# Moving the meta query's scores of a head from the head ahead (slots 4 to 6) into the head itself (slots 1 and 2)

## The chip, the core and the metric

The kernel runs on one core of one Trainium2 chip. The metric is the device time of one execution in microseconds (us); of several executions the median counts. The core has five engines with a queue each: TensorE (PE, with its weight loads shown apart as PEld), VectorE (DVE), ScalarE (ACT), GpSimd (POOL) and SyncE (SP), which here only issues DMAs. An engine runs its instructions in the order of the program and waits at semaphores for the others.

## What is computed

One layer of a bidirectional encoder over 1024 tokens with 16 meta tokens in front (1040 positions, 1024 features). Cut to the part that matters here:

```
q = rope(rmsnorm((rmsnorm(c_q) @ w_uq).reshape(B, T, 8, 96)))
k = rope(rmsnorm(concat(k_nope, k_rope)))           # 8 heads, 96 wide
s = einsum('bqhd,bkhd->bhqk', qblk, k) * scale      # T = 1040 keys
p = softmax(s, axis=-1)
y_mla = einsum('bhqk,bkhd->bqhd', p, v)
y = concat(rmsnorm(y_lru * gelu(g_lru)), rmsnorm(y_mla))
h = h + y @ w_out
gate, up = split(rmsnorm(h) @ w_ffn_up)
h = h + (silu(dwconv(gate)) * up) @ w_ffn_down
return h[:, 16:]                                     # meta rows are dropped
```

Only the 1024 token rows leave the layer, but the convolution over positions in the last part needs the row before the first token. That row is a meta position, so the attention also has to be done for the last meta tokens' queries; two of them are taken ("the meta query").

## The kernel before

The program has a projection and LRU part, an attention part (from about 245 to 535 us), the output projection, and the feed-forward part. The change is in the attention part, in `attention_out_phase`.

**Heads and slots.** There are 8 heads (0 to 7; END is 7) of 9 slots (0 to 8), one slot for each 128 keys; slot 8 holds the 16 meta keys. The loop `for h, s in steps` runs over heads and slots on PE, ACT and DVE alike. The numbers are fp32 split into a high and a low part, so each product takes three matmuls. In slot s PE makes

1. the scores of the keys of slot s against 512 queries (3 matmuls, L2027 to L2029), then a side job at place 0,
2. the scores against the other 512 queries (3 matmuls), then a side job at place 1,
3. the first half of the products with v of slot s-2 (3 matmuls, L2047, L2048, L2050; for slot 8 one matmul, L2044), then a side job at place 2,
4. the second half of these (3 or 1), then a side job at place 3.

ACT in slot s does the side jobs of places 0 and 1, in slot 1 the copy of the last head's output (`read_output`, o_sb, L1523), then two exponentials of the scores (e_f L1554 and e_h L1561; for slot 8 e_f, L1558 and L1559), and after them the side jobs of places 2 and 3. In slot 0 of heads 1 to 4 it also squares a part of y (L1482). DVE makes the low parts e_l of the last slot's exponentials (L1737, one for each half) between its share of the side jobs.

**Side jobs.** A side job writes one PSUM bank with PE, and ACT or DVE reads it. `PREPARE` lists them by slot and place, for head h+1 while head h runs: tq0, tq1, tk0, tk1 transpose q and k (four transposes each, L1907; ACT copies the high part, L1427, and then DVE makes the low part, L1141); a0 to a15 and am give the row maximum (one matmul L1922, DVE reduces it, L1699); tm transposes the meta rows (L1911, ACT L1437 and L1439); r transposes the maxima into a row (L1929), which ACT copies (L1448) and SP sends into row 96 of q_h. The scores of slot 0 wait for that row. x0, x1 and x2 are the meta query's scores: three matmuls each (L1941 to L1943), 2 rows against 512, 512 and 16 keys; ACT copies each into x_one (L1458); when x2 is copied, SP sends x_one to the head's rows of x_all (L1320). x_all is first read in slot 1 of head 7.

**Banks and waits.** In the heads the side jobs take two PSUM banks in turn, in the order of their list (`side_of`, `before`): the side job n waits on PE until the job n-2 has been read by its reader, which is ACT for x0, x1, x2 and r, and DVE for tq, tk and a. An a job also waits until ACT has copied the high parts of q and k of its head (`side_hi`). `read_output` waits for the last product of the last head, the second L2044 (`pv_done`).

**SP.** For each head SP has in its queue, in this order: (from head 1 on) the wait for x2 and x_all's DMA, the wait for r and the row's DMA, and `recip_row` of the last head (the sums' row out of o_sb as soon as o_sb is copied, L1162; then DVE's reciprocal at the end of slot 4; then two more DMAs).

Of the kernel before, what the change touches and what calls it, by code (L numbers as in the profile page):

```python
# [81 lines left out]
def f32(ap):  # L82
    return ap.bitcast(F32)
# [940 lines left out]
def attention_out_phase(nc, place, con, qk, v, yl, ym, res_t, x_h, x_l, up_raw, s_h, s_l, halo, bank, dram, sem):  # L1024
# [41 lines left out]
    def s_ps(g):  # L1066
# [7 lines left out]


    PREPARE = {0: ("tq0", "", "", "tq1"), 1: ("", "tk0", "", ""), 2: ("tk1", "", "a0", "a1"), 3: ("a2", "a3", "a4", "tm"),
               4: ("a5", "x0", "a6", "a7"), 5: ("a8", "x1", "a9", "a10"), 6: ("a11", "x2", "a12", "a13"),
               7: ("a14", "a15", "am", "r"), 8: ("", "", "", "")}
    FIRST = dict(PREPARE)
    FIRST.update({4: ("a5", "", "a6", "a7"), 5: ("a8", "", "a9", "a10"), 6: ("a11", "", "a12", "a13"), 8: ("x0", "x1", "x2", "")})  # L1080
    META_QUERIES = {5: ("xt", "", "", ""), 8: ("", "", "", "xo")}
    LRU_SUMS = {1: ("ys", "", "", "")}
    END = HEADS - 1
    NONE = ("", "", "", "")

    def side_jobs(h, s):

        places = [None] * 4
        for plan, head in [(FIRST if h < 0 else PREPARE, h + 1), (META_QUERIES, h), (LRU_SUMS, h)]:
            if 0 <= head < HEADS and not (plan is META_QUERIES and h != END) and not (plan is LRU_SUMS and h != END - 2):  # L1090
                for i, kind in enumerate(plan.get(s, NONE)):
                    if kind:
                        assert places[i] is None
                        places[i] = (kind, head)
        return places

    steps = [(h, s) for h in range(-1, HEADS + 1) for s in range(SLOTS)]
    jobs = [j for h, s in steps for j in side_jobs(h, s) if j]
    number = {j: n for n, j in enumerate(jobs)}
    first = len([j for s in range(SLOTS) for j in side_jobs(-1, s) if j])  # L1100
    BY_ACT = {"r", "x0", "x1", "x2"}
    LOWS = [("tq0", 0), ("tq1", 0), ("tk0", 0), ("tk1", 0)]
# [29 lines left out]
    def wait_read(eng, j):  # L1132

        same = [i for i in jobs[:number[j] + 1] if by_act(i) == by_act(j)]
        eng.wait_ge(sem["side_read_act" if by_act(j) else "side_read_dve"], len(same))
# [23 lines left out]
    def recip_row(eng, h):  # L1159

        eng.wait_ge(sem["o_read"], h + 1)
        eng.dma_start(rs, o_sb[VD:VD + 1].rearrange("p (a b) -> p a b", b=XT)).then_inc(sem["sums_in"], 16)  # L1162
        eng.wait_ge(sem["sums_recip"], h + 1)
        eng.dma_start(dram["recip"].rearrange("(a b) -> a b", b=XT), rs).then_inc(sem["recip_row"], 16)
        eng.wait_ge(sem["recip_row"], 16 * (h + 1))
        if h:
            eng.wait_ge(sem["y_mul"], h)
        eng.dma_start(rb, dram["recip"].unsqueeze(0).broadcast_to([VD, SEQ])).then_inc(sem["recip_in"], 16)
# [69 lines left out]
    def upto(kind, t):  # L1238

        return XT + 1 + GROUPS.index((kind, t)) + 1  # L1240
# [33 lines left out]
    def raw_of(m):  # L1274
        return raw03 if m == 3 else raw0[m % 4] if m < KD else raw1[m - KD]
# [35 lines left out]
    def sync(sp):  # L1311
        for h in range(HEADS):

            if h == END:
                sp.wait_ge(sem["ysum"], 4)
                for k in range(4):
                    sp.dma_start(raw_of(k), dram["w_out"][P * k:P * k + P, 0:half]).then_inc(sem["wo_a"][k], 16)
            def last_queries():
                wait_read(sp, ("x2", h))
                sp.dma_start(x_all[2 * h:2 * h + 2], x_one).then_inc(sem["x_in"], 16)  # L1320

            if h:
                last_queries()
            wait_read(sp, ("r", h))
            sp.dma_start(f32(q_h[h % 2][QK:QK + 1, 0:SEQ].rearrange("p (t n) -> p t n", n=P)), f32(r_row))\
              .then_inc(sem["row_in"], 16)
            if h == 0:
                last_queries()
            if h == END:
                sp.wait_ge(sem["side_done"], number[("tm", END)] + 1)  # L1330
                for i in range(4):
                    sp.dma_start(res_t[:, i, :], dram["x_tm"][P * i:P * i + P, :]).then_inc(sem["res_a"], 16)
            if h:
                recip_row(sp, h - 1)
        for i in range(4, XT):
            sp.dma_start(res_t[:, i, :], dram["x_tm"][P * i:P * i + P, :]).then_inc(sem["res_b"], 16)
        sp.wait_ge(sem["s_done"], SLOTS * END)
        for k in range(LF, KD):
            sp.wait_ge(sem["wo_lo"], k - LF + 1)
            sp.dma_start(raw0[k % 4], dram["w_out"][P * k:P * k + P, 0:half]).then_inc(sem["wo_a"][k % 4], 16)  # L1340
        sp.wait_ge(sem["s_done"], G)
        for k in range(LF):
            sp.dma_start(raw1[k], dram["w_out"][P * k:P * k + P, half:]).then_inc(sem["wo_in"][k], 16)
        recip_row(sp, END)

        sp.wait_ge(sem["wo_mm"], XT)
        sp.wait_ge(sem["wo_lo"], KD)
        for k in range(LF, KD):
            sp.dma_start(raw1[k], dram["w_out"][P * k:P * k + P, half:]).then_inc(sem["wo_a"][k - LF], 16)
        sp.dma_start(hm, dram["meta_tm"][META - 2:META, :]).then_inc(sem["res_in"], 16)  # L1350
        sp.dma_start(fg, dram["ffn_g"]).then_inc(sem["res_in"], 16)
        sp.wait_ge(sem["wo_lo"], 2 * KD)
        sp.dma_start(up_raw[:, 0, :], dram["w_up"][0, 0]).then_inc(sem["up_in"][0], 16)
        sp.wait_ge(sem["wo_mm"], upto("M", XT))
        for b in range(1, 4):
            sp.dma_start(up_raw[:, b, :], dram["w_up"][0, b]).then_inc(sem["up_in"][b], 16)
# [58 lines left out]
    def scalar(act):  # L1415
# [109 lines left out]
        for h, s in steps:  # L1525
# [10 lines left out]
            if h >= 1 and s == 2:  # L1536
                if h == HEADS - 1:

                    act.wait_ge(sem["x_max"], 1)
                    nc.scalar.activation(x_row, x_all, ACT.Exp, bias=x_v[QK:QK + NX, 3, 0:1], scale=SCALE)\  # L1540
                      .then_inc(sem["x_act"], 1)
            js = side_jobs(h, s)
            for j in js[0:2]:
                if j:
# [557 lines left out]
    def tensor_end(pe):  # L2102
        for n in blocks_in(NT)[1:]:
            transpose_block(pe, n)

    return {"sync": sync, "gpsimd": gpsimd, "scalar": scalar, "vector": vector, "tensor": tensor,
            "scalar_end": scalar_end, "tensor_end": tensor_end, "hn_meta": hn_m, "groups": ALL}

# [894 lines left out]
def build(nc, dram, out):  # L3003
    with ExitStack() as ctx:
# [21 lines left out]
        x_h, x_l, up_raw, s_h, s_l = norm_maps(place)  # L3026
        halo = place("halo", con["late"], (KD,))
        attention = attention_out_phase(nc, place, con, qk, v, yl, ym, h, x_h, x_l, up_raw, s_h, s_l, halo, bank, dram, sem)
        ffn = ffn_phase(nc, place, con, attention["hn_meta"], attention["groups"], h, x_h, x_l, up_raw, s_h, s_l, halo, bank, dram, out, sem)
        with nc.Block() as block:  # L3030
# [108 lines left out]
```

## Time and profile before

| | us |
|---|---|
| device time, median of 3 executions (lowest, highest) | 1303.34 (1301.97, 1305.87) |
| span of the profiled execution, first to last instruction | 1302.3 |
| PE busy in it | 1268.3 (97%) |
| DVE busy | 987.3 (76%) |
| ACT busy | 775.5 (60%) |
| POOL busy | 147.3 (11%) |
| share of PE in the chain that ended last | 86% |

The span leaves out what the chip does before the first and after the last instruction; the device time of the profiled execution itself is not listed apart, and the median of the executions is 1.0 us above its span. Busy time is the sum of an engine's instructions. Matmuls overlap: one of 512 columns is shown with some 0.39 us, but the next one begins 0.23 us after it. So PE's real pace is read from the starts, and the idle time in brackets in a timeline is counted from the modelled end of the matmul before it.

### The profile page before, as it was taken

The page shows a single profiled execution, that of the slowest core. Times are in us where ns is not written, and L with a number is a line of the kernel's source. Part 1 is how long each engine was busy: PE and PEld are TensorE (multiplying, and loading weights), DVE is VectorE, ACT ScalarE, POOL GpSimd, SP SyncE. Part 2 cuts the span into 40 slices and gives each one's busy share as a digit, 9 for nine tenths or more (in the row PEclk, how much of TensorE's full clock was granted, in tenths as well). Part 3 has the DMA queues.
Part 4 walks back from the last instruction along what each step waited for, and adds up shares of the span by engine and source line. Part 5 has one row for each costly group of instructions (what it writes and reads, how often), then busy time and mean ns, then how long its engine had stood idle before and what let it go on. Part 6 is the DMA issues. An engine that isn't in the chain of part 4 may idle for free.

```text
span 1302.3 us, 18506 instructions
## 1 busy us (share of the span) xinstructions
PE 1268.3 (97%) x6158; PEld 1015.7 (78%) x6158; DVE 987.3 (76%) x1498; ACT 775.5 (60%) x1163; POOL 147.3 (11%) x175
## 2 busy tenths in 40 slices
PE   7999999899999999999999999999999999999998
PEld 7999997666666666587678888888888888888886
DVE  6677569677777776577789887887878887887855
ACT  7487648567666776534445665656474665656460
POOL 3000037400000001232200000000010000000010
PEclk9999999999999999999999999999999999999999
DMA  6111200000000014210144847576674847575667
GB/s 220 35 52 41 74 1 1 1 2 9 9 9 10 9 42 170 62 37 1 37 148 103 190 97 169 112 170 133 158 165 93 193 97 169 110 169 132 161 138 250
DMA packets 40937, 123.00 MB, mean 94 GB/s; under 512 B 7378, under 2 KB 8082, under 8 KB 34484
## 3 DMA queue, kind: packets, MB, share of 16 engines
q0 software_dynamic: 7200, 52.43, 21.2%
q1 hardware_dynamic: 33684, 69.86, 15.5%
q8 instruction: 33, 0.54, 0.2%
q14 instruction: 20, 0.16, 0.0%
HBM read 62.34 MB, written 59.80 MB: 94 GB/s over the span
## 4 chain that ended last, share of the span: by engine, by line
PE 86%; ACT 5%; DVE 5%; issue 2%; DMA 1%; POOL 0%; SPq 0%; DVEq 0%; ACTq 0%; POOLq 0%
PE banks L2898 31%; PE banks L2970 15%; PE banks L100 7%; PE banks L102 7%; PE banks L101 7%; PE banks L1922 2%; PE banks L2027 2%; PE banks L2028 2%; PE banks L2029 2%; PE banks L2047 2%; PE banks L2050 2%; PE banks L2048 2%; ACT e_h L1561 1%; ACT e_f L1554 1%; PE banks L1882 1%
## 5 line engine op out<-in xcount | busy, mean ns | idle before, releaser
L2898 PE MATMUL banks<-x_hi,slot_h 128*128 128x512 f32 x616 | 242.9, 394 | 2.5 <-DVE slot_l L2586 1.3
L2898 PE MATMUL banks<-x_lo,slot_h 128*128 128x512 f32 x616 | 243.4, 395 | 0.0
L2898 PE MATMUL banks<-x_hi,slot_l 128*128 128x512 f32 x616 | 242.9, 394 | 0.0
L2371 ACT ACTIVATE slot_h<-up_raw 128x512 fp32r<-128x512 f32 x127 | 79.9, 630 | 174.2 <-PE banks L2898 173.5
L2898 PEld LDWEIGHTS banks<-x_hi,slot_h 128*128 128x128 f32 x616 | 115.6, 188 | 31.0 <-DVE slot_l L2586 2.3
L2898 PEld LDWEIGHTS banks<-x_lo,slot_h 128*128 128x128 f32 x616 | 115.7, 188 | 27.1
L2898 PEld LDWEIGHTS banks<-x_hi,slot_l 128*128 128x128 f32 x616 | 115.7, 188 | 26.9
L2449 ACT ACTIVATE staged<-banks 128x1024 f32<-128x1024 f32 x100 | 101.6, 1027 | 41.0 <-PE banks L2970 41.0
L2970 PE MATMUL banks<-dn_h,a_h 128*128 128x512 f32 x280 | 110.4, 394 | 0.0
L2970 PE MATMUL banks<-dn_h,a_l 128*128 128x512 f32 x280 | 109.5, 391 | 0.0
L2970 PE MATMUL banks<-dn_l,a_h 128*128 128x512 f32 x280 | 109.5, 391 | 0.0
L2354 POOL DMA_DIRECT2D down_sums<-staged x50 | 44.3, 886 | 570.3 <-ACT staged L2449 495.4
L1699 DVE TENSOR_REDUCE lam_t<-banks 128x1 f32<-128x512 f32 x128 | 85.3, 683 | 22.4 <-PE banks L1922 22.0
L100 PE MATMUL banks<-xn_h,win_h 128*128 128x346 f32 (+5 forms) x304 | 96.4, 317 | 1.5 <-DVE xn_l L669 1.5
L102 PE MATMUL banks<-xn_h,win_l 128*128 128x346 f32 (+5 forms) x304 | 95.2, 313 | 0.0
L101 PE MATMUL banks<-xn_l,win_h 128*128 128x346 f32 (+5 forms) x304 | 95.1, 313 | 0.0
L1554 ACT ACTIVATE e_f<-banks 128x1024 f32<-128x1024 f32 (+1 forms) x72 | 73.7, 1023 | 35.3 <-PE banks L2029 34.8
L1737 DVE TENSOR_TENSOR e_l<-e_f,e_h 128x512 fp32r<-128x512 f32 x128 | 88.0, 697 | 1.9 <-ACT e_h L1561 1.8
L2586 DVE TENSOR_TENSOR slot_l<-up_raw,slot_h 128x512 fp32r<-128x512 f32 x127 | 86.8, 684 | 3.2 <-ACT slot_h L2371 3.2
L2729 DVE SCALAR_TENSOR_TENSOR gate_conv<-gate,par,gate_conv 128x1024 f32<-128x1024 f32 x44 | 55.5, 1283 | 24.8 <-ACT gate_conv L2463 20.4
L1561 ACT ACTIVATE e_h<-banks 128x1024 fp32r<-128x1024 f32 x64 | 65.4, 1021 | 0.0
L1922 PE MATMUL banks<-k_h,q_h 96*128 96x512 f32 x128 | 54.8, 430 | 9.6 <-ACT k_h L1427 8.1
(345 smaller groups left out, 2848.2 us busy)
## 6 DMA issues: line engine op xcount, KB each, us to landing
down_sums<-staged POOLq DMA_DIRECT2D x50, 1024.0 KB, 8.0
up_raw<-in_w_up SPq DMA_DIRECT2D x88, 256.0 KB, 3.2
dn_raw<-in_w_down SPq DMA_DIRECT2D x22, 512.0 KB, 6.7
win_raw<-in_w_in SPq DMA_DIRECT2D x11, 512.0 KB, 3.3
x_tm<-in_x_tm SPq DMA_DIRECT2D x8, 512.0 KB, 6.0
wo_raw<-in_w_out SPq DMA_DIRECT2D x16, 256.0 KB, 4.2
h<-in_x_tm SPq DMA_DIRECT2D x8, 512.0 KB, 5.6
down_sums<-h SPq DMA_DIRECT2D x3, 1024.0 KB, 6.7
```

The source lines that it names most:

```text
L100: nc.tensor.matmul(out, w_h, x_h, start=first, stop=False)
L101: nc.tensor.matmul(out, w_h, x_l, start=False, stop=False)
L102: return nc.tensor.matmul(out, w_l, x_h, start=False, stop=last)
L1554: nc.scalar.activation(e_f[g % 3][0:n], s_ps(g)[0:n], ACT.Exp, scale=SCALE)
L1699: ins = nc.vector.tensor_reduce(mx3[:, i:i + 1], side, AX.X, ALU.max)
L1737: nc.vector.tensor_tensor(e_l[(g - 1) % 2][:, cs], e_f[(g - 1) % 3][:, cs], f32(e_h[(g - 1) % 3][:, cs]), ALU.subtract).then_inc(sem["e_lo ...
L1922: ins = nc.tensor.matmul(side, q_h[b][0:QK, tile_of(t)], k_h[b][0:QK, 512 * c:512 * c + 512], start=True, stop=True)
L2371: nc.scalar.activation(s_h[slot], x, ACT.Copy).then_inc(sem["up_hi"], 1)
L2449: nc.scalar.activation(staged[b][:, 2 * p:2 * p + 2, :], bank(4 + 2 * p, 2).rearrange("p (i n) -> p i n", i=2), ACT.Copy).then_inc(sem["dn ...
L2586: nc.vector.tensor_tensor(s_l[slot], x, f32(s_h[slot]), ALU.subtract).then_inc(sem["up_lo"], 1)
L2898: ins = nc.tensor.matmul(o, s[slot][:, k], xs[w], start=fresh and k == 0 and n == 0, stop=k == 3 and n == 2, skip_group_check=not fresh)
L2970: ins = nc.tensor.matmul(bank(4 + i), x[:, ts], w, start=k in FRESH and n == 0, stop=n == 2, skip_group_check=k not in FRESH)
```

## The change

x0, x1 and x2 of heads 1 to 6 leave places 1 of slots 4, 5 and 6 of the head ahead. They now stand in the head itself: x0 at place 2 and x1 at place 3 of slot 1, x2 at place 1 of slot 2. Head 0 (made ahead of the loop) and head 7 (made in slots 4 to 6 of head 6, `LAST_AHEAD`) stay as they were. The instructions are the same and as many as before. On SP the row's DMA of a head now stands ahead of x_all's DMA, and `recip_row` behind it.

```diff
     PREPARE = {0: ("tq0", "", "", "tq1"), 1: ("", "tk0", "", ""), 2: ("tk1", "", "a0", "a1"), 3: ("a2", "a3", "a4", "tm"),
-               4: ("a5", "x0", "a6", "a7"), 5: ("a8", "x1", "a9", "a10"), 6: ("a11", "x2", "a12", "a13"),
+               4: ("a5", "", "a6", "a7"), 5: ("a8", "", "a9", "a10"), 6: ("a11", "", "a12", "a13"),
                7: ("a14", "a15", "am", "r"), 8: ("", "", "", "")}
+    LAST_AHEAD = dict(PREPARE)
+    LAST_AHEAD.update({4: ("a5", "x0", "a6", "a7"), 5: ("a8", "x1", "a9", "a10"), 6: ("a11", "x2", "a12", "a13")})
     FIRST = dict(PREPARE)
-    FIRST.update({4: ("a5", "", "a6", "a7"), 5: ("a8", "", "a9", "a10"), 6: ("a11", "", "a12", "a13"), 8: ("x0", "x1", "x2", "")})
+    FIRST.update({8: ("x0", "x1", "x2", "")})
+    OWN = {1: ("", "", "x0", "x1"), 2: ("", "x2", "", "")}
...
-        for plan, head in [(FIRST if h < 0 else PREPARE, h + 1), (META_QUERIES, h), (LRU_SUMS, h)]:
+        ahead = FIRST if h < 0 else LAST_AHEAD if h == END - 1 else PREPARE
+        for plan, head in [(ahead, h + 1), (META_QUERIES, h), (LRU_SUMS, h), (OWN, h)]:
+            if plan is OWN and not 1 <= h < END:
+                continue
...
-            if h:
+            if h == END:
                 last_queries()
             wait_read(sp, ("r", h))
             sp.dma_start(f32(q_h[h % 2][QK:QK + 1, 0:SEQ].rearrange("p (t n) -> p t n", n=P)), f32(r_row))\
               .then_inc(sem["row_in"], 16)
-            if h == 0:
+            if h != END:
                 last_queries()
```

Line numbers after the change are 4 higher near PREPARE and 6 higher behind it.

PE, slots 1 and 2 of head 1, before (the transposes L1907 are tk0 and, in the second place, tk1; `side_read_dve` and `side_read_act` are the waits for a bank's reader):

```order
L1907 MATMUL banks<-ident,qk 96x128 [waits side_read_dve]
L1907 MATMUL banks<-ident,qk 96x128 x3
L2044 MATMUL banks<-e_meta,v_meta 66x512 [waits e_lo,e_hi]
L2044 MATMUL banks<-e_meta,v_meta 66x512 [waits e_lo]
L2027 MATMUL banks<-q_h_131,k_h_135 128x512 [waits e_hi]
L2028 MATMUL banks<-q_l_133,k_h_135 128x512
L2029 MATMUL banks<-q_h_131,k_l_137 128x512
L1907 MATMUL banks<-ident,qk 96x128 [waits side_read_dve]
```

and with the change (L1947 to L1949 are x0 and x1, L2050 is the product with v that was L2044, L1913 is tk1):

```order
L2050 MATMUL banks<-e_meta,v_meta 66x512 [waits e_lo,e_hi]
L1947 MATMUL banks<-k_h_135,q_h_131 2x512 [waits side_read_dve]
L1948 MATMUL banks<-k_h_135,q_l_133 2x512
L1949 MATMUL banks<-k_l_137,q_h_131 2x512
L2050 MATMUL banks<-e_meta,v_meta 66x512 [waits e_lo]
L1947 MATMUL banks<-k_h_135,q_h_131 2x512 [waits side_read_dve]
L1948 MATMUL banks<-k_h_135,q_l_133 2x512
L1949 MATMUL banks<-k_l_137,q_h_131 2x512
L2033 MATMUL banks<-q_h_131,k_h_135 128x512 [waits e_hi]
L2034 MATMUL banks<-q_l_133,k_h_135 128x512
L2035 MATMUL banks<-q_h_131,k_l_137 128x512
L1913 MATMUL banks<-ident,qk 96x128 [waits side_read_act]
```

Three matmuls of x0 now stand between the two products with v of slot 8, three of x1 behind them, and tk1's transposes wait for ACT (x0's copy), where they waited for DVE.

ACT, from the square in slot 0 to the exponentials of slot 2, before:

```order
L1482 ACTIVATE y_sq<-y_lru 128x1026
L1427 ACTIVATE k_h_136<-banks,par 96x512 [waits side_done]
L1523 ACTIVATE o_sb<-banks 66x1024 [waits y_mul,pv_done]
L1554 ACTIVATE e_f_145<-banks 128x1024 [waits pv_done,e_lo,s_done]
L1561 ACTIVATE e_h_140<-banks 128x1024
L1427 ACTIVATE k_h_136<-banks,par 96x512 [waits side_done]
L1554 ACTIVATE e_f_146<-banks 128x1024 [waits pv_done,e_lo,s_done]
L1561 ACTIVATE e_h_141<-banks 128x1024
```

and with the change:

```order
L1488 ACTIVATE y_sq<-y_lru 128x1026
L1433 ACTIVATE k_h_136<-banks,par 96x512 [waits side_done]
L1529 ACTIVATE o_sb<-banks 66x1024 [waits y_mul,pv_done]
L1560 ACTIVATE e_f_145<-banks 128x1024 [waits pv_done,e_lo,s_done]
L1567 ACTIVATE e_h_140<-banks 128x1024
L1464 ACTIVATE x_one<-banks 2x512 [waits x_in,side_done]
L1464 ACTIVATE x_one<-banks 2x512 [waits side_done]
L1433 ACTIVATE k_h_136<-banks,par 96x512 [waits side_done]
L1464 ACTIVATE x_one<-banks 2x16 [waits side_done]
L1560 ACTIVATE e_f_146<-banks 128x1024 [waits pv_done,e_lo,s_done]
L1567 ACTIVATE e_h_141<-banks 128x1024
```

Two copies of x_one now stand ahead of tk1's copy (the second k_h), and one ahead of slot 2's exponentials.

## Rows read from the trace of the kernel before

**Rows 1.** The page: each engine's busy time, share of the span and instructions
```profile
PE 1268.3 (97%) x6158; PEld 1015.7 (78%) x6158; DVE 987.3 (76%) x1498; ACT 775.5 (60%) x1163; POOL 147.3 (11%) x175
```

**Rows 2.** Who waited for whom: total us, times, longest us
```profile
PE banks L1922 <- ACT k_h L1427: 8.1, 8, 1.2
```

**Rows 3.** Timeline of PE, head 2, slots 1 to 3: start, us, instruction, idle before
```profile
319.27 0.60 PE L1907 MATMUL banks<-ident,qk 128*96 128x128 f32 x4
319.62 0.71 PE L2044 MATMUL banks<-e_meta,v_meta 80*66 80x512 f32 x2
...
322.48 0.40 PE L2050 MATMUL banks<-e_l,v 128*66 128x512 f32 x1
324.04 0.47 PE L1922 MATMUL banks<-k_h,q_h 96*128 96x512 f32 x1 [1.16 <-ACT k_h L1427]
324.35 0.40 PE L2047 MATMUL banks<-e_h,v 128*66 128x512 f32 x1
...
325.27 0.40 PE L2027 MATMUL banks<-q_h,k_h 97*128 97x512 f32 x1
...
325.97 0.46 PE L1922 MATMUL banks<-k_h,q_h 96*128 96x512 f32 x1
...
329.19 0.26 PE L1911 MATMUL banks<-ident,qk 16*96 16x16 f32 x2
```

**Rows 4.** Timeline of ACT, head 2, slots 1 and 2
```profile
319.91 0.69 ACT L1427 ACTIVATE k_h<-banks,par 96x512 fp32r<-96x512 f32 x1
320.49 1.01 ACT L1523 ACTIVATE o_sb<-banks 66x1024 f32<-66x1024 f32 x1
321.40 1.02 ACT L1554 ACTIVATE e_f<-banks 128x1024 f32<-128x1024 f32 x1
322.30 1.02 ACT L1561 ACTIVATE e_h<-banks 128x1024 fp32r<-128x1024 f32 x1
323.21 0.69 ACT L1427 ACTIVATE k_h<-banks,par 96x512 fp32r<-96x512 f32 x1
```

**Rows 5.** Timeline of DVE, head 2, slots 1, 2 and 4
```profile
320.62 0.75 DVE L1141 SCALAR_TENSOR_TENSOR k_l<-banks,par,k_h 96x512 fp32r<-96x512 f32 x1 [0.19 <-ACT k_h L1427]
...
323.93 0.75 DVE L1141 SCALAR_TENSOR_TENSOR k_l<-banks,par,k_h 96x512 fp32r<-96x512 f32 x1 [0.82 <-ACT k_h L1427]
...
324.60 0.68 DVE L1737 TENSOR_TENSOR e_l<-e_f,e_h 128x512 fp32r<-128x512 f32 x1
325.20 0.68 DVE L1699 TENSOR_REDUCE lam_t<-banks 128x1 f32<-128x512 f32 x1
...
334.76 0.19 DVE L1758 RECIPROCAL sum_cols<-sum_cols 128x8 f32<-128x8 f32 x1
```

**Rows 6.** Timeline of PE, head 2, slots 4 and 6: x0 and x2, and what follows
```profile
331.12 0.39 PE L1941 MATMUL banks<-k_h,q_h 96*2 96x512 f32 x1
...
331.81 0.40 PE L2047 MATMUL banks<-e_h,v 128*66 128x512 f32 x1
...
339.50 0.17 PE L1941 MATMUL banks<-k_h,q_h 96*2 96x16 f32 x1
...
339.58 0.42 PE L2047 MATMUL banks<-e_h,v 128*66 128x512 f32 x1
```

**Rows 7.** Timeline of ACT ahead of head 0: the copies of x0, x1, x2
```profile
245.65 1.34 ACT L1458 ACTIVATE x_one<-banks 2x512 f32<-2x512 f32 x3 [0.43 <-PE banks L1943]
```

**Rows 8.** Timeline of DVE and PE, head 0, slot 2: transposes that wait
```profile
252.22 0.75 DVE L1141 SCALAR_TENSOR_TENSOR q_l<-banks,par,q_h 96x512 fp32r<-96x512 f32 x1 [1.78 <-ACT q_h L1427]
...
253.02 0.64 PE L1907 MATMUL banks<-ident,qk 128*96 128x128 f32 x4 [0.40 <-DVE q_l L1141]
253.42 0.48 PE L2027 MATMUL banks<-q_h,k_h 97*128 97x512 f32 x1
...
254.20 0.40 PE L2047 MATMUL banks<-e_h,v 128*66 128x512 f32 x1
```

**Rows 9.** Timeline of SP's queue, head 2: the sums' row out of o_sb
```profile
321.53 0.53 SPq L1162 DMA_DIRECT2D sum_cols<-o_sb  x1
```

## The prediction

> **What bounds the kernel now.** I read the page's busy line first: PE is busy for 97% of the span, the others for 76% and less [rows 1]. So the question is only what the change does to PE: its instructions stay the same, and what can change is the time in which it stands still. The waits view names one regular pause in the heads: PE waits at L1922 for ACT's copy of k_h, 8 times, 8.1 us, never over 1.2 us [rows 2]. The timelines of one head, 2, show where. The first max job a0 starts at 324.04, while the product with v before it started at 322.48 and its successor could have followed after 0.23 us, at 322.71: PE loses 1.33 us there [rows 3]. It waits for tk1's copy, which started at 323.21 and ends at 323.90 [rows 4]. Ahead of that copy ACT runs four instructions without a gap: tk0's copy 319.91, o_sb 320.49, e_f 321.40, e_h 322.30 [rows 4]. So between slot 1 and a0 **ACT is the late engine**; elsewhere in the head PE goes on at its own pace. Each of heads 1 to 6 has this one pause, and by the 1.2 at most in the waits row none has a longer one [rows 2]. The change puts 1.5 us of PE work just into this stretch, but also two copies on ACT, and that is what the sum is about.
>
> **What the change takes away.** In slots 4 and 5 of the head ahead, x0 and x1 each hold PE for 331.81 - 331.12 = 0.69 us; in slot 6, x2 holds it for 339.58 - 339.50 = 0.08, and the product behind these short ones starts a little late, so I take 0.10 [rows 6]. Together 1.48, say **-1.49 us** for each of six heads, if PE stays the late engine there. DVE is the cover to check: with three max jobs and two e_l it has 5 steps in a slot, 0.60 us from start to start (324.60 to 325.20, rows 5), 3.0 us, and PE's slot without an x job is 12 + 3 matmuls of 0.23, 3.5 us. It fits with 0.5 us to spare. ACT's two exponentials (0.91 apart, rows 4) leave still more.
>
> **What it adds, step by step, in head 2's times.**
>
> 1. x0 stands between the two L2044. The first half holds PE from 319.62 for 0.28, x0's matmuls take 319.90 to 320.59, and the second L2044, which ended at 319.62 + 0.71 = 320.33, now ends at 321.02 [rows 3, 6].
> 2. `read_output` waits for that one. o_sb started at 320.49 and now starts at 321.05: **+0.56** on ACT's chain. Then e_f at 321.96 and e_h at 322.86, by the spacings of 0.91 and 0.90 [rows 4]; e_h ends at 323.88.
> 3. x0's copy. Three x copies took 1.34 us, of which the small one is under 0.2: 0.59 for each large one, one behind the other with no overlap, where other copies start 0.1 before the end of their predecessor [rows 4, 7]. I let x0's copy start only when e_h has ended: 323.89 to 324.48. x1's follows to 325.07.
> 4. On PE, x1 needs tk0's bank, which DVE leaves at 320.62 + 0.75 = 321.37 [rows 5]; from a release by DVE to PE's start I take 0.09, as between 325.20 + 0.68 and 325.97 [rows 3, 5]. x1 runs to 322.24, the scores of slot 2 to 322.94. These waits lie beside ACT's chain and cost nothing of their own.
> 5. tk1's transposes now wait for x0's copy, 324.48, and start at 324.53: in head 0 the same wait took 253.02 - (252.22 + 0.75) = 0.05 [rows 8]. PE stands still for 1.6 us here. The transposes end 0.64 later, at 325.17, and the next scores start 0.40 after them, at 324.93; these take 0.78 [rows 8], x2 0.08, the product with v behind it 0.73 (three matmuls 0.69, and the late start): PE is ready for a0 at 326.52.
> 6. tk1's copy on ACT: 325.21 to 325.90. a0 now stands two places behind tk1 in the list of side jobs and uses its bank, so it also waits for DVE's low part: 325.93 to 326.68 (0.75, rows 5). a0 starts at 326.77, against 324.04: 2.73 us later. Behind it the pace is as before (0.31 to the next, rows 3).
> 7. Slot 3 then starts at 328.00, against 325.27. Before, it lasted 329.19 - 325.27 = 3.92 us, because DVE was still catching up on e_l and max jobs after the late start [rows 3]. Now DVE is ahead when it begins: 12 matmuls of scores and products and 3 of max jobs at 0.23 make 3.49. That gives back **-0.43**.
>
> The sum for one head is 2.73 - 0.43 - 1.49 = **+0.81 us**: the move costs 1.49 of PE work in the new place and returns it in the old one, but the single pause of 1.3 us becomes two of 1.6 and 0.25. Six heads: **+4.9 us**. The profiled span of 1302.3 would become 1307.2; against the median of 1303.34 the time is **1308.2 us**, +0.37%.
>
> **SP at no cost.** The sums' row was sent at 321.53 and is used by DVE at 334.76 [rows 5, 9]. Now it stands behind x2's copy (at about 325.9 to 326.1) and the x_all DMA, so it goes some 5 us later, at about 326.8, and some 8 us are left for a DMA of 4 KB, of which I know here only that its issue takes 0.53. Without that cover, DVE would stop at its reciprocal in slot 4. The r row goes first in the queue now and is not behind any new wait. x0's copy waits for the last head's x_all DMA, which is most of a head old; for head 7 it is two slots old.
>
> **Bounds.** If slot 3 gives nothing back, a head costs 1.24 and the total is +7.4 us (1310.8). If o_sb were not held up by x0 (its +0.56), a head costs 0.25 and the total is +1.5 us (1304.8). Between these I stay at 0.81, since the o_sb wait is in the instruction order and the catching up is in the rows. For the overlap of step 3 the row of three x copies shows none [rows 7]. The Trainium skill ("ScalarE: Activation LUTs", section "What ACT_TABLE_LOAD costs") says that back-to-back ACTIVATEs overlap by about 93 ns; by that rule, an estimate, x0's copy would be ready 0.09 earlier in each head and the total 0.6 us less. The k_h, o_sb and e rows follow that rule, the x copies among themselves do not.
>
> **Rivals.**
>
> - *The pause is filled* (faster). PE has 1.33 us of nothing before a0, and 1.48 us of x work are put ahead of it; if ACT's two copies fell beside PE's work, the pause and slot 3's catching up would both vanish: 6 x (1.33 + 0.43) = 10.6 us less, 1292.7. For it speaks that the idle time is there and of the right size. Against it: it is ACT that is late there, and the change gives ACT 1.18 us more ahead of just the copy that PE waits for. Chance 0.09.
> - *A shorter chain* (about no change): o_sb isn't held up, or the copies overlap more than I let them; +0.25 a head, 1304.8. Against it the second L2044 ended only 0.16 before o_sb's start, so 0.69 more must show. Chance 0.19.
> - *Slots 4 to 6 give nothing like 1.49 back* (slower still). Without the x job, DVE becomes the late engine. The one slot of the trace with three max jobs and no x job is slot 3, at 3.92 us instead of 3.49 [rows 3]; if slots 4 to 6 also took 3.92, each would cost 0.43 more: 6 x 3 x 0.43 = 7.7 on top, 1315.9. It decides from the point at which DVE's slot passes 3.5 us; its five steps make 3.0. Chance 0.08.
> - *The change doesn't do what it says*: the instruction order shows the x jobs of heads 1 to 6 in the new places, so I give it nothing.
>
> **How the numbers follow.** My forecast has a chance of 0.64, with its own range of 1306.3 to 1310.8. A difference under 0.3% (3.9 us) can't be told from no change in a measurement of this kernel; the forecast is 1.0 us beyond that, so of its 0.64 I count 0.12 as within 0.3%. Slower: 0.52 + 0.08 = 0.60. The same: 0.12 + 0.19 = 0.31. Faster: 0.09. The range from 1303.5 to 1311.5 takes in the forecast, its bounds and the shorter chain, and leaves out 0.09 + 0.08 = 0.17.
>
> **What would show it.** In the profile after: the second of the two products with e_meta ends 0.7 us later, and o_sb starts 0.5 to 0.6 later against tk0's transposes; the x copies come right behind e_h; tk1's transposes are released by ACT's x_one after an idle time of some 1.4 us (from the modelled end), six times; a0 is released by DVE's k_l, with an idle time of 0.1 to 0.2; the wait of L1922's successor for k_h's copy is gone in heads 1 to 6; slot 3 lasts 3.5 us, and slots 4 to 6 too, with no idle time of PE. A whole head takes 0.8 us more. I am wrong if tk1's transposes start without a wait, if o_sb keeps its place against tk0, or if PE shows pauses in slots 4 to 6.

## The result: slower by twice as much as forecast

The changed kernel takes 1313.04 us (median of 5 executions, 1311.37 to 1318.41), the kernel before 1303.34: ratio 1.008, 95% interval 1.0065 to 1.0095. The way was forecast, the size was not: +9.7 us against +4.9, and 1313 lies above the range. The profiled span went from 1302.3 to 1311.1 us, +8.8.

The profile after, first the page's lines that answer to [rows 1] and the waits that answer to [rows 2]:

```profile
span 1311.1 us, 18506 instructions
PE 1272.2 (97%) x6158; PEld 1018.4 (78%) x6158; DVE 989.5 (75%) x1498; ACT 776.3 (59%) x1163; POOL 146.9 (11%) x175
PEld banks L1913 <- ACT x_one L1464: 12.1, 6, 2.1
PE banks L1913 <- ACT x_one L1464: 9.6, 6, 1.6
PEld banks L1947 <- DVE k_l L1147: 5.3, 6, 0.9
```

The wait of a0 for k_h is no longer among them in heads 1 to 6; in its place tk1's transposes (L1913) wait six times for x_one, as forecast. But PE's busy time rose by 3.9 us, with as many instructions as before. Waits don't raise it: some matmuls got slower.

Timeline of PE, head 2, slots 1 and 2, to be read against [rows 3] (start, us, instruction, idle before):

```profile
319.88 0.60 PE L1913 MATMUL banks<-ident,qk 128*96 128x128 f32 x4
320.24 0.48 PE L2050 MATMUL banks<-e_meta,v_meta 80*66 80x512 f32 x1
...
321.25 0.39 PE L2050 MATMUL banks<-e_meta,v_meta 80*66 80x512 f32 x1
322.06 0.39 PE L1947 MATMUL banks<-k_h,q_h 96*2 96x512 f32 x1 [0.42 <-DVE k_l L1147]
...
325.18 0.64 PE L1913 MATMUL banks<-ident,qk 128*96 128x128 f32 x4 [1.57 <-ACT x_one L1464]
...
327.38 0.50 PE L1928 MATMUL banks<-k_h,q_h 96*128 96x512 f32 x1
...
328.64 0.40 PE L2033 MATMUL banks<-q_h,k_h 97*128 97x512 f32 x1
...
332.23 0.26 PE L1917 MATMUL banks<-ident,qk 16*96 16x16 f32 x2
```

and of ACT, against [rows 4] and [rows 7]:

```profile
320.54 0.69 ACT L1433 ACTIVATE k_h<-banks,par 96x512 fp32r<-96x512 f32 x1
321.68 1.02 ACT L1529 ACTIVATE o_sb<-banks 66x1024 f32<-66x1024 f32 x1 [0.46 <-PE banks L2050]
322.60 1.01 ACT L1560 ACTIVATE e_f<-banks 128x1024 f32<-128x1024 f32 x1
323.50 1.01 ACT L1567 ACTIVATE e_h<-banks 128x1024 fp32r<-128x1024 f32 x1
324.54 1.06 ACT L1464 ACTIVATE x_one<-banks 2x512 f32<-2x512 f32 x2
325.86 0.68 ACT L1433 ACTIVATE k_h<-banks,par 96x512 fp32r<-96x512 f32 x1 [0.26 <-PE banks L1913]
```

This head starts 0.61 us later than before (tk0 at 319.88 for 319.27). With that taken off, o_sb starts at 321.07 (forecast 321.05), tk1 at 324.57 (324.53), a0 at 326.77 (326.77), slot 3 at 328.03 (328.00). The chain is as it was worked out.

The length of the heads, from one r job (L1929, now L1935) to the next, shows what is missing:

| head | 0 | 1 | 2 | 3 | 4 | 5 | 6 |
|---|---|---|---|---|---|---|---|
| before, us | 32.26 | 34.39 | 34.38 | 34.41 | 34.33 | 37.03 | 34.78 |
| changed, first profile | 30.78 | 36.54 | 35.29 | 36.60 | 35.28 | 37.96 | 38.35 |
| changed, second profile | 30.73 | 36.58 | 36.49 | 35.36 | 36.44 | 39.21 | 38.81 |

(Each column runs from the start of the head's own r job to that of the next one's, so it begins at slot 7 of the head ahead. "First profile" is that of the result, "second profile" that of e12 below.) Head 0 is 1.48 shorter, since it lost x(1); head 6 holds two heads' x jobs and is 1.5 longer for that. Heads 2 and 4 of the first profile cost 0.91 to 0.95 each. Heads 1 and 3, and 6, cost 1.2 us more than that. The windows view has the reason in its column of the granted clock (the number behind POOL's):

```profile
core 0: us, PE busy (x) PEld busy (x) DVE busy (x) ACT busy (x) POOL busy (x), PEclk, DMA share, GB/s
286.00:290.00 4.00, 2.42 (x16) 1.65 (x15) 0.11 (x1) 3.72 (x6) 0.00 (x0) 1.00 0.00 0
290.00:294.00 4.00, 4.00 (x15) 2.51 (x12) 3.20 (x5) 2.17 (x4) 0.00 (x0) 0.57 0.03 3
322.00:326.00 4.00, 2.37 (x12) 1.52 (x13) 1.74 (x3) 3.72 (x6) 0.00 (x0) 1.00 0.00 0
326.00:330.00 4.00, 3.94 (x20) 2.58 (x19) 3.43 (x6) 2.65 (x4) 0.00 (x0) 1.00 0.03 3
358.00:362.00 4.00, 2.41 (x16) 1.62 (x15) 1.16 (x2) 3.64 (x7) 0.00 (x0) 0.99 0.00 0
362.00:366.00 4.00, 4.00 (x12) 2.57 (x11) 3.16 (x5) 2.06 (x3) 0.00 (x0) 0.59 0.03 5
```

Right behind the pauses of head 1 (window 290 to 294) and of head 3 (362 to 366) **TensorE's clock fell to 1.2 GHz for a while** and came back to 2.4; behind the same pause of head 2 (326 to 330) it did not. (A window's number is a mean over both levels.) While the clock is low, matmuls of 512 columns follow each other every 0.43 us, not every 0.23; in head 1:

```profile
291.06 0.64 PE L1928 MATMUL banks<-k_h,q_h 96*128 96x512 f32 x1
291.49 0.63 PE L2053 MATMUL banks<-e_h,v 128*66 128x512 f32 x1
291.92 0.63 PE L2054 MATMUL banks<-e_h,v 128*64 128x512 f32 x1
```

In the profile before the change no head shows it. The same two windows of head 1 stand at 1.00, with PE busy for 2.83 of the first 4 us where it is now busy for 2.42:

```profile
286.00:290.00 4.00, 2.83 (x15) 1.84 (x14) 1.85 (x4) 4.00 (x6) 0.00 (x0) 1.00 0.02 1
290.00:294.00 4.00, 3.99 (x18) 2.52 (x16) 4.00 (x8) 2.56 (x4) 0.00 (x0) 1.00 0.02 4
```

So the 8.8 us of the profile are 6 x 0.92 = 5.5 for the chain and 3 x 1.2 = 3.6 for three falls of the clock, 9.1 in all, less 0.3 elsewhere. The theory to test has two parts: (a) ACT's chain, (b) the clock. The rivals: the loss is one mechanism (the waits) and the clock only goes with it; or the new places cost through the head they are in, SP's order or the buffers.

### The profile page after: what moved, and what is told of

Read it like the earlier page. It is cut to its first block, busy times and chain, and to the rows that moved or that the text cites. A ratio compares the mean times of both kernels' runs of the same rounds, so it can differ in the third digit from the quotient of the medians.

```text
span 1311.1 us, 18506 instructions
## 1 busy us (share of the span) xinstructions
PE 1272.2 (97%) x6158; PEld 1018.4 (78%) x6158; DVE 989.5 (75%) x1498; ACT 776.3 (59%) x1163; POOL 146.9 (11%) x175
## 4 chain that ended last, share of the span: by engine, by line
PE 86%; ACT 5%; DVE 5%; issue 1%; DMA 1%; POOL 0%; SPq 0%; DVEq 0%; POOLq 0%
PE banks L2904 31%; PE banks L2976 15%; PE banks L100 7%; PE banks L102 7%; PE banks L101 7%; PE banks L1928 2%; PE banks L2033 2%; PE banks L2053 2%; PE banks L2034 2%; PE banks L2035 2%; PE banks L2054 2%; PE banks L2056 2%; ACT e_f L1560 1%; ACT e_h L1567 1%; PE banks L1888 1%
## 5 line engine op out<-in xcount | busy, mean ns | idle before, releaser
L2683 DVE TENSOR_TENSOR dn_l<-dn_raw,dn_h 128x512 fp32r<-128x512 f32 x70 | 48.0, 686 | 20.1 <-ACT dn_h L2441 20.0
```

## Experiments

The kernel before was timed again beside each group: 1302.43 (29 executions) for e1 to e4, 1302.83 (29) for e5 to e8, 1303.87 (17) for e9 to e12.

### The pause filled with work

```diff
                 if 0 <= g < G:
                     scores(g, c)
+                if c == 0 and s == 2 and 1 <= h < END:
+                    for _ in range(12):
+                        nc.tensor.matmul(bank(2 * (g % 2) + 1)[:, 0:P], ident, ident, start=True, stop=True)
                 place_job(h, s, js, c)
```

> The changed kernel with 12 matmuls of 128 columns (ident times ident, into a bank that is free there) behind the first scores of slot 2 in heads 1 to 6, just where PE waits for x0's copy. They add PE work of about 1.5 us (16 such took 2.03 us before head 0) into a pause of 1.7 us, and change no wait. Theory, clock: the changed kernel's profile shows 1.2 GHz in heads 1, 3 and 6 right behind this pause, and each such head lasts 1.2 us longer than the others; with the pause filled the clock stays at 2.4 GHz in all heads. Then every head lasts 35.3 us (37.3 for head 5, with the LRU sums), the span is about 3.6 us under that of the changed kernel (1307.5), and the time about 5.5 us over the kernel before: 1308.9, ratio 1.004. Rival, the clock falls whatever PE does in the pause, or what is lost is in the waits: 1313, ratio 1.008. Rival, the fillers delay PE: above 1313.

1317.88 us, ratio 1.0104 (1.0081 to 1.0126). The fillers were twice as long as meant: the trace shows 24 of them in 2.84 us, so PE came to tk1 1.0 us after x0's copy was ready, and heads 1 to 3 last 36.2 us. The clock half came out as expected: no stretch at 1.2 GHz in any head. So it is a slower kernel with a full clock (the expectation had 1308.9), and e5 takes 7 fillers in place of 12.

> The changed kernel with fillers in the same pause as in e1_fill_pause, but sized by that run's trace: each of the 12 was shown as two of 0.12 us, so they took 2.7 us and held PE 1 us past the pause. Now 7 of them, 14 x 0.12 = 1.65 us, against a pause of 1.73. Theory, clock: no head falls to 1.2 GHz, every head of 1 to 4 lasts 35.3 us, and the time is 0.92 us a head above the kernel before: +5.5 us, 1308 against 1302.4, ratio 1.004, lower than the changed kernel's 1.008. Rival, clock without a part in it: ratio 1.008.

1310.73 us, **ratio 1.0052 (1.0038 to 1.0067)**: adding some 10 us of useless matmuls (14 of 0.12 us, in six heads) made the changed kernel faster: it stood at 1.008 (1.0065 to 1.0095; this interval and e5's just touch) and in e12, below, at 1.0096 (1.0081 to 1.011). The six heads from head 1 on last 35.31, 35.31, 35.32, 35.27, 40.35 and 37.17 us: the 35.3 of the chain alone in all of 1 to 4, and 37.2 in head 6 where the changed kernel had 38.35 and 38.81. The mean clock of e5's six executions is 0.993 to 0.997, that of the changed kernel's nine 0.987 to 0.993. The clock by windows:

```profile
286.00:292.00 6.00, 5.94 (x37) 4.33 (x35) 2.01 (x4) 5.62 (x9) 0.00 (x0) 1.00 0.02 4
322.00:328.00 6.00, 5.91 (x37) 4.39 (x36) 3.13 (x5) 5.34 (x8) 0.00 (x0) 1.00 0.02 2
424.00:434.00 10.00, 10.00 (x48) 7.40 (x47) 3.05 (x7) 5.09 (x7) 0.00 (x0) 0.66 0.00 0
468.00:474.00 6.00, 5.93 (x37) 4.41 (x36) 2.20 (x4) 5.60 (x8) 0.00 (x0) 1.00 0.01 2
```

Only head 5 falls (424 to 434), though PE has no idle time there. It is the head with the LRU sums' 18 matmuls of 2 columns in slot 1. The same fall, beginning at 422 and 424, stands in two kernels whose head 5 has no x job in slots 1 and 2 (e3, e6), so it isn't the change's; the expectation of a full clock in every head was wrong there, and with it the time: 1310.73 for the expected 1308. In head 5 e5 is slower than the changed kernel (40.35 for 37.96 and 39.21).

> The kernel before with 5 fillers (10 x 0.12 = 1.2 us) ahead of a0 in heads 1 to 6, where PE pauses 1.33 us for tk1's copy; they go into a0's own bank when it is free. Theory: the clock of the kernel before does not fall for this pause in its profile, so the heads keep their 34.4 us and the time is that of the kernel before, ratio 0.999 to 1.0005. If its pause does cost clock in a part of the executions (they spread from 1300.5 to 1307.3), the median falls by 0.5 to 1.5 us and the spread narrows. Rival, fillers cost time of their own: ratio 1.002 or more.

1303.11 us, ratio 1.0006 (0.9992 to 1.002). Heads 1 to 4 last 34.38, 34.37, 34.39, 34.39 us, as without fillers: in these profiles the pause before the change costs no clock in them, and fillers inside a wait cost nothing themselves. Head 5 falls here (39.16 us), as said above. The kernel before isn't free of falls in every execution: its mean clock is 0.993 to 0.999 over its 75 timings beside the experiments.

### A longer pause without any work moved

```diff
             js = side_jobs(h, s)
+            if s == 2 and 1 <= h < END:
+                nc.scalar.activation(full[0], full[0], ACT.Copy)
             for j in js[0:2]:
```

> The kernel before, with one more copy on ACT (96x512, SBUF to SBUF, some 0.55 us) ahead of tk1's copy in slot 2 of heads 1 to 6; no PE work is moved or added. Theory, ACT's chain sets a0: the pause ahead of a0 grows from 1.33 to about 1.9 us and each head by 0.5 to 0.6: +3.3 us. Theory, clock: with a longer pause of PE the clock falls to 1.2 GHz behind it in some of the heads, each of them 1 to 1.5 us more; in all 1306.5 to 1311, ratio 1.0025 to 1.006, with the lost clock in the heads of the profile. Without the clock's part: 1306.6, ratio 1.0025, all heads at 2.4 GHz. Rival, ACT has slack there: 1303.3.

1307.09 us, ratio 1.0037 (1.0024 to 1.0049). Waits of a0 (here L1924) for k_h's copy:

```profile
PE banks L1924 <- ACT k_h L1427: 10.1, 8, 1.7
```

The pause grew to 1.83 to 1.85 us (1.33 before), and heads 1, 3 and 4 to 35.05, 34.92 and 34.92 (+0.5 to +0.7): what ACT is later comes back in the head's length. Head 2 lasts 36.12, with the clock at 0.54 and 0.61 in the windows 324 to 326 and 326 to 328. Head 5 falls too, at 426, ahead of its pause, which is 0.78 us there.

Then two copies in the place of the one, the second waiting for the first, and the same with 9 fillers (18 as the trace counts them) ahead of a0:

```diff
+            if s == 2 and 1 <= h < END:
+                for m in range(2):
+                    if h > 1 or m:
+                        act.wait_ge(sem["ident_in"], 16 + 2 * (h - 1) + m)
+                    nc.scalar.activation(full[0], yl[0:QK, 3, 0:512], ACT.Copy).then_inc(sem["ident_in"], 1)
...
+                if kind == "a0" and 2 <= h <= END:
+                    for _ in range(9):
+                        nc.tensor.matmul(side[:, 0:P], ident, ident, start=True, stop=True)
                 pe.wait_ge(sem["side_hi"], hi_upto(j))
```

> The kernel before, with two more copies on ACT (96x512, 0.55 us and a wait for one another) ahead of tk1's copy in slot 2 of heads 1 to 6; no work of PE added. Theory, chain: the pause ahead of a0, 1.33 us before and 1.83 with one copy, becomes about 2.5 us in each head. Theory, clock: 1.33 showed no stretch at 1.2 GHz in heads 1 to 4 and 6, 1.83 showed it in one of these; with 2.5 it comes in most of them, each costing 1 to 1.5 us beyond the pause. Time: +1.2 x 6 = 7.2 for the chain and 3 to 8 for the clock: 1313 to 1318, ratio 1.008 to 1.012. Without the clock's part: 1309.8, ratio 1.0055.

> As e10_two_copies, and PE fills the pause ahead of a0 in these heads with 9 fillers (18 x 0.12 = 2.1 us). The waits and ACT's chain are those of e10. Theory, clock: what e10 loses beyond 1.2 us a head is the stretch at 1.2 GHz behind the pause, and PE's work in the pause keeps the clock up: ratio 1.0055 to 1.006, under e10 by what its profile shows at 1.2 GHz in heads 1 to 4 and 6. Rival, the loss is the wait alone: e11 and e10 are the same.

e10: 1315.53 us, ratio 1.0086 (1.0073 to 1.0099). e11: 1312.15 us, ratio 1.0064 (1.005 to 1.0078). The waits are the same, and so are the heads without a fall: e10's head 2 lasts 35.56 us, and e11's heads 1 to 4 last 35.56, 35.54, 35.60 and 35.60. e10's heads 1, 3 and 4 last 38.12, 36.86 and 36.77, all with the clock down behind the pause, head 1 over a longer stretch. Heads 5 and 6 fall in both kernels: head 5 ahead of the pause (at 433 in e10, at 429 in e11), head 6 in e10 behind the pause. In e11 head 6 keeps the clock behind the filled pause and loses it at the end of slot 6, where PE waits for ACT without fillers in the wait, after ACT had waited 3.6 us for a DMA of w_out's weights; this head lasts 41.38 us:

```profile
490.69 0.80 PE L1930 MATMUL banks<-k_h,q_h 96*128 96x512 f32 x1 [1.93 <-ACT x_one L1458]
```

Windows of e10, heads 1, 2 and 3:

```profile
288.00:298.00 10.00, 7.67 (x21) 5.10 (x20) 5.64 (x9) 6.06 (x8) 0.00 (x0) 0.66 0.01 2
326.00:332.00 6.00, 3.66 (x15) 2.20 (x14) 4.00 (x7) 4.52 (x7) 0.00 (x0) 1.00 0.01 1
362.00:370.00 8.00, 5.80 (x18) 4.22 (x19) 5.24 (x10) 5.03 (x8) 0.00 (x0) 0.79 0.01 1
```

and of e11, heads 1 and 2:

```profile
288.00:294.00 6.00, 5.77 (x33) 4.17 (x32) 3.88 (x7) 4.53 (x7) 0.00 (x0) 1.00 0.01 0
324.00:330.00 6.00, 5.72 (x30) 3.98 (x29) 4.34 (x8) 4.52 (x7) 0.00 (x0) 1.00 0.00 0
```

This is the pair that parts (a) from (b), in the kernel before and with nothing of the change in it: the intervals of the two totals overlap a little (1.0078 and 1.0073), heads 1 to 4 of the profiles do not. The mean clocks of the single executions are 0.988 to 0.995 for e10 and 0.993 to 0.997 for e11. By the profiles of the unfilled kernels, a pause of 1.33 us cost no clock in heads 1 to 4 and 6, 1.83 in one of these five (head 2), 2.5 in four (1, 3, 4, 6), and the changed kernel's 0.57 and 1.74 close together in three and, in its second profile, in four. Head 6 of e2 and of e3, below, is left as changed and falls behind its pause in both, so this pair of pauses was followed by a fall in 9 of 12 heads. Filled, the pauses were followed by none in 15: heads 1 to 4 and 6 of e1, e5 and e11.

### The changed kernel again

> The changed kernel once more, on the same chip as e10 and e11 and for a second profile. Theory: pauses as in the first profile (0.56 and 1.74 us more than PE's pace in each of heads 1 to 6), heads without a stretch at 1.2 GHz last 35.3 us (head 5: 37.9), heads with one 1.2 us more; how many heads have one differs from execution to execution, so the single times spread over some 5 us, and their differences go with the mean granted clock. Median ratio 1.007 to 1.008. Rival, the 1.2 GHz stretches stand in fixed heads (1, 3 and 6): the second profile shows them there again.

Median 1316.25 us of 4, ratio 1.0096 (1.0081 to 1.011), above the expected 1.007 to 1.008. The pauses are the same (0.55 to 0.58 and 1.72 to 1.76), but now heads 1, 2, 4, 5 and 6 fall and head 3 does not (35.36 in the table above). Windows behind the pause of heads 2, 3 and 4:

```profile
326.00:328.00 2.00, 2.00 (x6) 1.13 (x6) 1.36 (x4) 1.64 (x2) 0.00 (x0) 0.50 0.05 6
358.00:364.00 6.00, 4.39 (x23) 2.71 (x22) 3.16 (x5) 5.45 (x8) 0.00 (x0) 1.00 0.01 3
398.00:400.00 2.00, 2.00 (x6) 1.13 (x6) 1.23 (x3) 1.63 (x2) 0.00 (x0) 0.50 0.05 6
```

So the heads that fall are not the same each time, though heads 1 and 6 did in both. A fall costs 36.5 - 35.3 = 1.2 us; the longer ones (head 1 of e10, head 6 of e2 and e3) cost 2.6 to 2.8. The single times go with the mean clock: the changed kernel's five executions were 1311.4 to 1313.0 at a mean clock of 0.993, and 1317.7 and 1318.4 at 0.989 and 0.987; the four of this run 1313.9 at 0.992 and 1316.1 to 1316.5 at 0.991 and 0.990.

### Other places for the x jobs

```diff
+    OWN_15 = {1: ("", "", "", "x0"), 2: ("", "x1", "", ""), 4: ("", "x2", "", "")}
-        ... (OWN, h)]:
+        ... (OWN_15 if h < END - 1 else OWN, h)]:
```

> The changed kernel, but in heads 1 to 5 x0 stands at place 3 of slot 1 (behind both products with v of slot 8), x1 at place 1 of slot 2, x2 at place 1 of slot 4, and SP sends x_all's rows behind the sums' three DMAs. Head 6 stays as changed. Theory, ACT's chain: o_sb keeps its start (not held up by x0), only one copy stands ahead of tk1's, and tk1's transposes wait for nothing; x1 waits for x0's copy instead, about 1.2 us, beside the same chain. By the same step-by-step account as the prediction's a head of these costs about 0.4 us less than before the change: five heads -2.0, head 6 +0.9 (and +1.2 more if the clock falls there): 1302 to 1303.5, ratio 0.999 to 1.000. Rival, any x work between tk0 and a0 costs its time: 1308 or more, ratio 1.004.

In the head itself, x0 and x1 stand one position later than in the change and x2 in slot 4; on SP, x_all's DMA stands behind the sums' DMAs (lines not shown). 1304.38 us, ratio 1.0006 (0.9991 to 1.0021). Heads 1 to 4 last 34.15, 34.10, 34.16 and 34.12: 0.25 **less** than before the change, with x0 and x1 still between tk0 and a0 but one position later. o_sb is not held up, tk1 doesn't wait, and the one pause is in front of x1:

```profile
322.81 0.40 PE L1950 MATMUL banks<-k_h,q_h 96*2 96x512 f32 x1 [1.14 <-ACT x_one L1467]
```

Head 6, left as changed, lasts 39.74 (37.2 without a fall, by e5) and takes the gain away.

```diff
+    OWN_15 = {4: ("", "x0", "", ""), 5: ("", "x1", "", ""), 6: ("", "x2", "", "")}
```

> The changed kernel, but in heads 1 to 5 x0, x1 and x2 stand at place 1 of slots 4, 5 and 6 of the head itself, one head later than before and in the same places of a slot, with SP's x_all DMA behind the sums' three. Only head 6 has them in slots 1 and 2 as changed. Theory: it is the place in the slots that costs, not the head: heads 1 to 5 last 34.4 us as before, head 6 0.9 longer, and 1.2 more where the clock falls: 1304.2 to 1305.5, ratio 1.001 to 1.002. Rival, x in the head itself costs by another way (SP's order, the buffers of q and k): 1308 and more.

1304.18 us, ratio 1.0007 (0.9993 to 1.0021), heads 1 to 4 at 34.37, 34.32, 34.48, 34.32: in the head itself, but in slots 4 to 6, x costs what it cost before. So it is not the head that matters, and the rival on the head and its buffers falls. SP's order differs from the change's here too, so e3 doesn't test it; the profile of the change does. There the sums' row is sent at 327.47 and DVE's reciprocal starts without a wait (no idle time ahead of it):

```profile
337.08 0.19 DVE L1764 RECIPROCAL sum_cols<-sum_cols 128x8 f32<-128x8 f32 x1
```

Head 6 of e3 again carries the cost, 39.98.

### A version that beats both

Since the pause came from tk1's copy standing behind o_sb and two exponentials, tk0 and tk1 move ahead of them (from the kernel before, x jobs untouched):

```diff
-    PREPARE = {... 1: ("", "tk0", "", ""), 2: ("tk1", "", "a0", "a1"), ...
+    PREPARE = {... 1: ("tk0", "tk1", "", ""), 2: ("", "", "a0", "a1"), ...
-    LRU_SUMS = {1: ("ys", "", "", "")}
+    LRU_SUMS = {1: ("", "", "ys", "")}
```

> The kernel before with tk0 and tk1 at places 0 and 1 of slot 1 (before: tk0 at place 1 of slot 1, tk1 at place 0 of slot 2), so that tk1's copy stands ahead of o_sb and the two exponentials on ACT and not behind them; the LRU sums' job of head 5 moves from place 0 to place 2 of slot 1. No work is added. Theory, ACT's chain tk0, o_sb, e_f, e_h, tk1 is what a0 waits for: a0 then waits for nothing, tk1 waits some 0.3 us for tq1's bank. A head loses its 1.33 us pause and 0.4 in slot 3, gains 0.3: 33.0 us for 34.4, six to seven heads: -8 us, 1294.5, ratio 0.994. Rival, the wait only moves (o_sb and the exponentials 0.6 us later hold the products with v of slot 2 or the scores of slot 3): ratio 0.998 to 1.000.

1300.80 us, **ratio 0.9982 (0.9973 to 0.9991)**: faster than the kernel before by about 2 us and than the changed one by 12. But 8 us were expected. The pause at a0 is gone; heads 2 to 4 last 34.07, 34.11 and 34.02 us and not 33.0. A good part of the wait has moved: a2 now waits for DVE, 0.71 us late, and slot 3 lasts 4.87 us for 4.10. In these heads DVE has the sum of squares in its way:

```profile
323.62 1.22 DVE L1639 TENSOR_TENSOR y_sum<-y_sum,y_sq 128x1026 f32<-128x1026 f32 x1
...
326.09 0.50 PE L1922 MATMUL banks<-k_h,q_h 96*128 96x512 f32 x1 [0.55 <-DVE lam_t L1699]
```

The sum is the smaller part of it. Head 1 has no sum in slot 1 and lasts 33.83; there a2 is still 0.47 us late and slot 3 lasts 4.62. DVE's low parts follow ACT's exponentials, which start later behind the two copies. No head shows a fall of the clock.

In e8 the square moves from slot 0 to slot 4 (`if 1 <= h <= LF and s == 4`) and its sum to slot 5:

> As e7_tk1_early, and the square of y in heads 1 to 4 moves from slot 0 to slot 4 on ACT, its sum on DVE from slot 1 to slot 5. Theory: in slots 8 to 2 ACT is the late engine of these heads, and its 0.97 us square stands in that stretch; without it tk0's and tk1's copies come up to 0.9 us earlier. If e7 still shows waits for ACT in heads 1 to 4 and none in head 6, this takes them away: up to 0.5 us in each of 4 heads, ratio 0.001 to 0.002 under that of e7. Rival, ACT catches up in slot 1 anyway: the same time as e7.

1302.29 us, ratio 0.9992 (0.9983 to 1.0002), 0.001 above e7: the sum holds up a max job in slot 5 for 0.5 us (heads 2 to 4 at 34.4). In e9 only the sum moves, to slot 8:

> As e7_tk1_early, and DVE's sum of squares in heads 2 to 4 (1.2 us) moves from slot 1 to slot 8, where DVE was seen idle for 2.4 us. In e7's trace a2 waits 0.71 us for DVE in heads 2 to 4, which have the sum in slot 1, and 0.46 in heads 1, 5 and 6, which have not. Theory: the sum is what makes the difference, so heads 2 to 4 go from 34.05 to 33.8 us, and the time is 0.8 us under e7: ratio to the kernel before 0.9976. Rival: it is late somewhere else and the time is e7's, 0.9982, or over it as in e8.

1301.70 us, ratio 0.9986 (0.9973 to 0.9998). Heads 1 to 4 last 33.81 us as expected, the shortest of all kernels, but the total can't be told from e7's: this profile has head 5 at 37.25 with a fall of the clock at 425 to 429, and a fall in head 0, at 248, which e7 hasn't.

## Why the prediction came out wrong

**Right, by its steps.** What the chain needs of steps 1 to 6 was met within 0.05 us in head 2 (above): o_sb +0.58 for +0.56, tk1 released by x0's copy, a0 behind DVE's low part of tk1, 2.73 us later as forecast. Step 4 ended 0.1 too late by a slip in its sum (321.46 + 0.69 is 322.15, not 322.24), so PE's pause ahead of tk1 was 1.7 us and not 1.6; the chain doesn't run through it. What the old places return was 1.5 as taken: slots 4, 5 and 6 now last 3.6, 3.5 and 3.5 us with no idle time of PE, so DVE's cover held, and that rival is out. The filled pause, the rival that would have made it faster, is out: two pauses stand where one was. SP's later DMA cost nothing; DVE's reciprocal stood in its old place at the end of slot 4.

**One term was a tenth off.** A head without a fall costs 0.92 us, not 0.81. Slot 3 lasts 3.59, not 3.49, as PE is still a little late at tm; it gives back 0.33 for the 0.43 of step 7. That is 0.6 us in six heads. By this alone the time would have been 1303.34 + 6 x 0.92 = 1308.9, inside the range.

**The step that failed** is the sum itself: it priced PE's matmuls at their starts of 0.23 us apart wherever they stand, as if the clock were fixed. The granted clock was in the profile (1.00 in every head) and was read as given. The pauses I had worked out, 0.6 and 1.6 us close together in the place of one of 1.3, are what stood ahead of each fall, and none of my rivals named this. Three falls in the first profile and five in the second, at 1.2 us, make 3.6 and 6 us. In the first profile that is all that is missing of the span; of e12's median (1316.25, at a lower clock than its profile) about 1 us stays without a count. e5 (filled, heads 1 to 4 back at 35.3) and e10 against e11 show the clock as the cause and not as something that goes with the waits. e4 fits, with one head.

**The row on the copies was misread.** From the three x copies ahead of head 0 [rows 7] I took that they never overlap. But the row is a sum of three: the second had waited 0.11 us for PE, and the third did start 0.09 before the second ended. In the changed kernel x1's copy starts 0.09 before x0's ends as well, which agrees with the 93 ns that the Trainium skill gives ("ScalarE: Activation LUTs", "What ACT_TABLE_LOAD costs"). But x0's copy does not overlap with e_h: 323.50 + 1.01 = 324.51, start 324.54. Since x0's end sets tk1, that rule of the Trainium skill would have been wrong by 0.1 where it counted, and the prediction's start of x0's copy came out right by luck: its row doesn't show what was taken from it.

On the clock, the Trainium skill ("TensorE: Matmul & The Clock Gate", section "Why this matters for your kernels") warns of drops in mid-kernel after idle gaps between bursts of matmuls, and names gaps longer than any between two matmuls of these heads (2.5 us in e10). A pause of 1.74 us with one of 0.57 ahead of it was enough in this kernel, in 3 and 5 of 6 heads: the measurement decides. That activity brings the clock back, as the Trainium skill says ("TensorE: Matmul & The Clock Gate", section "What's actually happening"), agrees with the return to 1.00 in the windows.

**Left open.** Which head falls differs from one profile to the next, and no run here shows what decides it. Nor was it tried what makes head 5 fall in kernels that leave it alone. Its 2-column matmuls are a suspicion: in seven of the fourteen profiles (e3 to e6, e9 to e11) the clock falls within 1.5 us of their end, with PE shown as busy; in the other seven it doesn't. No run drops them (e7 to e9 move them by two places, and e9 falls). In e6:

```profile
421.54 1.96 PE L1988 MATMUL banks<-ones,y_sum 128*128 128x2 f32 x18
...
424.24 0.89 PE L1907 MATMUL banks<-ident,qk 128*96 128x128 f32 x4
```

It isn't shown either whether the short pause of 0.57 us counts in the changed kernel, or the long one alone: no run has 1.74 without it.

## What to carry to other kernels

Before moving PE work into a stretch where PE waits, ask what the late engine has to do for that work: here two small copies on ACT and one product held up cost more than the free PE time gave, and the same work one position later (e2) cost nothing. Where a change makes PE pause longer, even by half a microsecond, price the clock as well: look at the granted clock behind the longest pause of the profile, and test with fillers inside the wait, which cost nothing there if they are shorter than it. When a pause on the bound engine comes from the order on another one, reorder that one (e7) before filling the pause, and look for where the wait goes: here only 2 us of 8 came.

## What the runs showed of the hardware

- The clock can fall behind PE pauses under 2 us. In the four profiles with an unfilled pause of 1.7 us or more in each of heads 1 to 4 and 6 (the changed kernel's two, e4, e10), one to four of these five heads fell behind it, and a fall cost 1.2 us of the head (36.5 for 35.3): matmuls of 512 columns start every 0.43 us while it lasts. With fillers in the pause (e1, e5, e11) none of 15 fell.
- Matmuls of ident by ident (fp32, 128 columns) are shown as two each, 0.12 us apiece: a filler of 12 was 24.
- x0's copy (2x512, into x_one) starts 0.02 us after e_h's end in all six heads of the changed kernel, where e_h starts 0.1 before the end of e_f; what makes the difference wasn't tried.
- The row's DMA that slot 0 waits for is nearly always just in time, but held PE up for 0.6 us in one head of e1 and for 0.9 us in one of e6:

```profile
417.06 0.50 PE L2030 MATMUL banks<-q_h,k_h 97*128 97x512 f32 x1 [0.91 <-DMA q_h<-r_row]
```
